# Two-layer streaming encoder step on one core: the embedding blocks' operands split into high and low parts

## The reference, cut to what matters

```python
def mixer_layer(h, p, ...):                       # two layers; 512 prompt frames and 8 x 16 sample frames
    z = rmsnorm(h, ln_in) @ w_in                  # 1024 -> 2464 columns: queries, latents, gates, conv inputs
    # o_a: latent attention, 8 heads; v: causal depthwise conv, width 31
    ...
    y_a = rmsnorm(o_a * silu(g_a), ln_out_a)
    v = silu(layernorm(v, ln_conv_g, ln_conv_b))
    y_c = rmsnorm(v * silu(g_c), ln_out_c)
    h = h + concatenate([y_a, y_c], axis=-1) @ w_out      # 1024 -> 1024
    gate = sigmoid(rmsnorm(h, ln_pg) @ w_pg)
    h = h + gate * (p @ w_pe)                             # p: 256 columns, the layer's input embedding
```

## Time and profile before

| | |
|---|---|
| three runs, us | 765.39, 765.08, 766.03 (median 765.39) |
| the profiled execution | 765.02 us, span 762.9 us |
| busy: TensorE / VectorE / ScalarE / GpSimd | 749.0 / 562.0 / 428.2 / 91.6 us |
| instructions | 10602 |
| TensorE's granted clock, mean | 0.996 of full |
| DMA | 70.69 MB, 92 GB/s to and from HBM over the span |

### The profile page before, as it was taken

One profiled execution on the slowest core, in us unless ns is written; L12 is line 12 of the kernel. 1 busy time (PEld: TensorE's weight loads), 2 busy tenths in 40 slices (PEclk: granted clock), 3 DMA queues, 4 the chain that ended last, 5 costly groups with the idle time before them and its releaser, 6 DMA issues.

```text
span 762.9 us, 10602 instructions
## 1 busy us (share of the span) xinstructions
PE 749.0 (98%) x3749; PEld 601.8 (79%) x3749; DVE 562.0 (74%) x1084; ACT 428.2 (56%) x996; POOL 91.6 (12%) x161
## 2 busy tenths in 40 slices
PE   9999999999999999999999999999999999999995
PEld 7899887767777588888888988877678767888874
DVE  3459978979877986546453798988888879655577
ACT  3865655665566733263366575647655758223564
POOL 1500323420001400000000020353000000000000
PEclk9999999999999999999999999999999999999998
DMA  8742222410011343412282223233111014332203
GB/s 271 229 128 83 88 73 86 115 36 15 35 35 28 123 167 130 134 56 83 66 279 77 91 76 85 82 81 83 41 36 43 1 54 154 110 125 74 88 5 138
DMA packets 50681, 70.69 MB, mean 93 GB/s; under 512 B 15582, under 2 KB 28154, under 8 KB 50614
## 3 DMA queue, kind: packets, MB, share of 16 engines
q1 hardware_dynamic: 44746, 59.27, 24.6%
q0 software_dynamic: 5824, 10.73, 5.2%
q10 hardware_dynamic: 60, 0.02, 0.0%
HBM read 60.79 MB, written 9.27 MB: 92 GB/s over the span
## 4 chain that ended last, share of the span: by engine, by line
PE 89%; DVE 6%; ACT 2%; DMA 1%; issue 1%; SPq 0%; POOL 0%; ACTq 0%
PE acc L692 20%; PE acc L701 20%; PE acc L698 19%; PE sharedT L616 5%; PE acc L836 5%; PE sharedS L930 4%; PE sharedO L944 4%; PE sharedO L616 2%; PE sharedS L616 2%; DVE VT L1623 2%; PE sharedT L902 1%; PE sharedS L888 1%; PE sharedO L874 1%; PE sharedS L889 1%; PE sharedO L913 1%
## 5 line engine op out<-in xcount | busy, mean ns | idle before, releaser
L692 PE MATMUL acc<-WHI,XHI 128*128 128x512 f32 (+1 forms) x710 | 304.7, 429 | 0.8 <-ACT WHI L1115 0.5
L701 PE MATMUL acc<-WHI,XLO 128*128 128x512 f32 (+1 forms) x710 | 274.7, 387 | 0.0
L698 PE MATMUL acc<-WLO,XHI 128*128 128x512 f32 (+1 forms) x710 | 274.3, 386 | 0.0
L1623 DVE SCALAR_TENSOR_TENSOR VT<-UX,CWT,VT 128x640 f32<-128x640 f32 x240 | 211.5, 883 | 5.0
L692 PEld LDWEIGHTS acc<-WHI,XHI 128*128 128x128 f32 x710 | 133.7, 188 | 29.8 <-issue 6.2
L1553 DVE SCALAR_TENSOR_TENSOR WLO<-WR,GT,WHI 128x512 fp32r<-128x512 f32 (+1 forms) x142 | 98.7, 737 | 78.8 <-ACT WHI L1115 78.6
L698 PEld LDWEIGHTS acc<-WLO,XHI 128*128 128x128 f32 x710 | 133.9, 189 | 27.3 <-issue 6.2
L701 PEld LDWEIGHTS acc<-WHI,XLO 128*128 128x128 f32 x710 | 133.3, 188 | 26.2
L1115 ACT ACTIVATE WHI<-WR,GT 128x512 fp32r<-128x512 f32 (+1 forms) x142 | 93.4, 708 | 85.5 <-PE acc L701 85.3
L1336 ACT ACTIVATE SB<-SB,NBIAS 128x128 f32<-128x128 f32 (+2 forms) x80 | 44.4, 555 | 37.0 <-DVE NBIAS L1682 35.6
L1115 ACT ACTIVATE PT<-sharedT 128x384 f32<-128x384 f32 (+1 forms) x80 | 35.6, 444 | 37.1 <-PE sharedT L616 36.9
(11 more groups left out here) (213 smaller groups left out, 884.4 us busy)
## 6 DMA issues: line engine op xcount, KB each, us to landing
WR<-in_w_in_dram SPq DMA_DIRECT2D x32, 256.0 KB, 3.1
WR<-in_w_in_dram SPq DMA_DIRECT2D x16, 512.0 KB, 3.7
WR<-in_w_out_dram SPq DMA_DIRECT2D x16, 512.0 KB, 3.7
WR<-in_w_pg_dram SPq DMA_DIRECT2D x16, 512.0 KB, 3.5
H<-in_x_prompt_dram SPq DMA_DIRECT2D x16, 256.0 KB, 5.2
WR<-in_w_in_dram SPq DMA_DIRECT2D x8, 416.0 KB, 5.8
residual_spill<-H SPq DMA_DIRECT2D x5, 512.0 KB, 3.4
H<-residual_spill SPq DMA_DIRECT2D x10, 256.0 KB, 3.4
```

What stands on the lines that cost most here:

```text
L692: mm(out, hi, w_hi, start=(first and k == 0), stop=False)
L698: mm(out, hi, w_lo, start=False, stop=False)
L701: last = mm(out, lo, w_hi, start=False, stop=(final and k == 1))
L1623: stt(out=out, in0=src, scalar=w, in1=out, op0=ALU.mult, op1=ALU.add).then_inc(conv_done, 1)
```

## The change

- `pe0` and `pe1` become quanta like all others: their chunks are parts (no gain), split by ScalarE and VectorE, and their inputs are split into rows 4 and 5 of `XHI` and `XLO`, which are free once part 2 of `gc` has been used. Three fp32r matmuls take the place of each plain one.
- The high parts of the inputs are two copies of 128x640 by ScalarE in unit 22; the low parts two subtractions of 128x640 by VectorE in units 27 and 29.
- `pe1` moves behind `oa0`. Parts are renumbered in each layer: 20 is `pe0`, 21 and 22 `oa0`, 23 `pe1`, 24 and 25 `oa1`, and so on, two higher than before from `oa1` on. Part 20 and 21 are split in the units 28 to 31.
- The turns of `y_a` stand between the tiles of `pe0` and of `oa0`'s first half.
- VectorE's and ScalarE's work after the attention is put in another order, and the table of taps is changed in "turn" and units 0, 2, 3, 24, 27.
- The load of a chunk waits for the split of the one three before, for `pe` too.

```diff
-BLOCKS = ["u0", "zA", "u1", "ga", "gc", "cv", "pe0", "pe1", "oa0", "oa1", "oc0", "oc1", "pg0", "pg1"]
+BLOCKS = ["u0", "zA", "u1", "ga", "gc", "cv", "pe0", "oa0", "pe1", "oa1", "oc0", "oc1", "pg0", "pg1"]
...
-PARTS = [c for c in CHUNKS if c[1][:2] != "pe"]
+PARTS = CHUNKS
...
-TAP["turn"] = _take(1)
-
-for _u, _m in enumerate((2, 1, 0, 4, 1, 1, 4, 2, 1, 2, 0, 2, 1, 1, 4, 2, 1, 2, 0, 2, 1, 1, 4, 1, 0, 1, 1, 3)):
+TAP["turn"] = _take(2)
+
+for _u, _m in enumerate((1, 1, 1, 3, 1, 1, 4, 2, 1, 2, 0, 2, 1, 1, 4, 2, 1, 2, 0, 2, 1, 1, 4, 1, 1, 1, 1, 2)):
     TAP[NB + _u] = _take(_m)
...
+        def first_x(name):
+
+            return 2 if name[:2] == "pe" else first_rows(name)
+
         def gain_column(i, k):
             l, name, c = PARTS[i]
+            if name[:2] == "pe":
+                return None
             col = G_IN if name in ZCOL else G_OUT if name[0] == "o" else G_PG
             col += 2 * (c + first_rows(name)) + k
             return GT[:, l, col:col + 1]
...
-                    pl, name, c = before = CHUNKS[j - RAW]
-                    if before in PART:
-                        sp.wait_ge(split_ready, PART[before] + 1)
-                    else:
-                        sp.wait_ge(acc_filled[TILES - 1], BLK[pl, name] + 1)
+                    before = CHUNKS[j - RAW]
+                    sp.wait_ge(split_ready, PART[before] + 1)
                 load_piece(sp, j)
...
-                    row = 2 * (c + first_rows(name)) + k
+                    row = 2 * (c + first_x(name)) + k
...
-
-            def embed(half, t, ks=(0, 1)):
-
-                j = CHUNK[l, f"pe{half}", 0]
-                if t == 0 and 0 in ks:
-                    raw_wait(pe, j)
-                if 0 in ks:
-                    pe.wait_ge(acc_drained[t], BLK[l, f"pe{half}"])
-                for k in ks:
-                    last = mm(acc[t][:, :], PTR[:, k, P * t:P * (t + 1)], WR[:, j % RAW, k, :],
-                              start=(k == 0), stop=(k == 1))
-                if 1 in ks:
-                    last.then_inc(acc_filled[t], 1)
...
-            copied_wait(pe, (l, "p2"))
-            embed(0, 0)
+            pe.wait_ge(p_low, 2 * (l + 1))
+            quantum("pe0", 0, 0)
             values(UNITS - 1)
-            for t in range(1, TILES):
-                embed(0, t)
-            embed(1, 0)
 
             def turn_ya(t):
                 pe.wait_ge(ya_ready, TILES * l + t + 1)
                 flip_half((l, ("y", t, 0)), Y[:, t, :])
 
             for t in range(1, TILES):
-                embed(1, t)
-                turn_ya(t - 1)
+                quantum("pe0", 0, t)
+                if t > 1:
+                    turn_ya(t - 2)
             for c in range(2):
                 for t in range(TILES):
                     copied_wait(pe, (l, ("y", t, 0)))
                     quantum("oa0", c, t)
-                    if (c, t) == (0, 0):
-                        turn_ya(TILES - 1)
+                    if c == 0 and t < 2:
+                        turn_ya(t + 3)
+            for t in range(TILES):
+                quantum("pe1", 0, t)
             for c in range(2):
                 for t in range(TILES):
...
+            def embeddings_high():
+
+                part_used(act, PART[l, "gc", 2])
+                for k in range(2):
+                    copy(XHI[:, :, 4 + k, :], PTR[:, k, :].rearrange("p (t e) -> p t e", e=P)).then_inc(p_high, 1)
...
                 split_high(NB + u)
+                if u == 22:
+                    embeddings_high()
+                if u in (28, 30):
+
+                    high(first_i + 20 + (u - 28) // 2)
...
             act.wait_ge(conv_done, CONVS * (l + 1))
-            for t in range(TILES):
-                embedding_out(0, t)
-                if t == 2:
-                    high(first_i + 20)
-            v_tanh_out(0)
-            for t in range(TILES):
+
+            def ya_square(t):
                 act.wait_ge(ya_ready, TILES * l + t + 1)
                 mean_square(Y[:, t, 0:512], 15 + t, 512)
+
+            embedding_out(0, 0)
+            embedding_out(0, 1)
+            ya_square(0)
+            embedding_out(0, 2)
+            high_half((l, ("y", 0, 0)))
+            ya_square(1)
+            embedding_out(0, 3)
+            high_half((l, ("y", 1, 0)))
+            embedding_out(0, 4)
+            high_half((l, ("y", 2, 0)))
+            high(first_i + 22)
+            high_half((l, ("y", 3, 0)))
+            ya_square(2)
+            high_half((l, ("y", 4, 0)))
+            ya_square(3)
+            ya_square(4)
+            v_tanh_out(0)
+            v_tanh_out(1)
+            high(first_i + 23)
+            v_tanh_out(2)
+            v_tanh_out(3)
+            for t in range(TILES):
+                embedding_out(1, t)
+                if t == 0:
+                    high(first_i + 24)
                 if t == 1:
-                    v_tanh_out(1)
-                embedding_out(1, t)
-                if t:
-                    high_half((l, ("y", t - 1, 0)))
-            high(first_i + 21)
-            high_half((l, ("y", TILES - 1, 0)))
-
-            for t in (2, 3, 4):
-                v_tanh_out(t)
+                    v_tanh_out(4)
             for t in range(TILES):
                 act.wait_ge(yc_ready, TILES * l + t + 1)
                 mean_square(Y[:, t, 512:1024], 20 + t, 512)
-            high(first_i + 22)
-            high(first_i + 23)
+            high(first_i + 25)
             for t in range(TILES):
...
-            for i in range(25, 28):
+                    high(first_i + 26)
+            for i in range(27, 30):
...
+                    if gain_column(i, k) is None:
+                        out = tt(split_place(i, 1, k, n), raw[:, k, :], split_place(i, 0, k, n).bitcast(F32), ALU.subtract)
+                        continue
...
+                if u in (27, 29):
+
+                    k = (u - 27) // 2
+                    dve.wait_ge(p_high, 2 * l + k + 1)
+                    tt(XLO[:, :, 4 + k, :], PTR[:, k, :].rearrange("p (t e) -> p t e", e=P),
+                       XHI[:, :, 4 + k, :].bitcast(F32), ALU.subtract).then_inc(p_low, 1)
+                if u >= 30:
+
+                    low(first_i + u - 10)
                 for t in CONV_OUT.get(u, ()):
                     conv_stats(t)
             sample_heads_out()
-            norm_of_conv()
             head_out(HEADS - 1)
             copied_wait(dve, (l, ("oh", HEADS - 1)))
             copied_wait(dve, (l, "oa"))
...
             for t in range(TILES):
                 y = Y[:, t, 0:512]
                 tt(y, y, OTOK[:, t, :], ALU.mult).then_inc(ya_ready, 1)
-            norm_of_conv_end()
-            for t in range(TILES):
-                normed(t)
-                if t == 2:
-                    low(first_i + 20)
-
             def conv_gate(t):
 
                 v = VT[:, 512 * t:512 * (t + 1)]
...
 
 
             low_half((l, ("y", 0, 0)))
+            norm_of_conv()
+            low_half((l, ("y", 1, 0)))
+            low_half((l, ("y", 2, 0)))
+            norm_of_conv_end()
+            low(first_i + 22)
+            low_half((l, ("y", 3, 0)))
+            normed(0)
+            low_half((l, ("y", 4, 0)))
+            normed(1)
             conv_gate(0)
-            for t in (1, 2, 3):
-                low_half((l, ("y", t, 0)))
-            conv_gate(1)
-            low_half((l, ("y", 4, 0)))
-            low(first_i + 21)
-            for t in (2, 3, 4):
-                conv_gate(t)
+            normed(2)
 
             def norm_of_y(group):
...
             norm_of_y(0)
-            low(first_i + 22)
+            low(first_i + 23)
             for t in range(TILES):
                 onto_residual("oa0", t)
-            low(first_i + 23)
+                if t in (1, 2):
+                    conv_gate(t)
+                    normed(t + 2)
+            low(first_i + 24)
+            conv_gate(3)
+            conv_gate(4)
+            low(first_i + 25)
             norm_of_y(1)
             for t in range(TILES):
                 low_half((l, ("y", t, 1)))
                 if t == 0:
-                    low(first_i + 24)
+                    low(first_i + 26)
                 if t > 1:
                     onto_residual("oa1", t - 2)
             onto_residual("oa1", 3)
             onto_residual("oa1", 4)
-            low(first_i + 25)
-            low(first_i + 26)
+            low(first_i + 27)
+            low(first_i + 28)
...
```

More of the change, by code:

```diff
@@ L311, in build @@
         p_in = sem("p_in")
+        p_high = sem("p_high")
+        p_low = sem("p_low")
         wq_rot = sem("wq_rot")
@@ L1471, in scalar_layer @@
                 if t == 0:
-                    high(first_i + 24)
-            for i in range(25, 28):
+                    high(first_i + 26)
+            for i in range(27, 30):
                 high(first_i + i)
@@ L1478, in scalar_layer @@
                 high_half((l, ("h", t, 0)))
-            high(first_i + 28)
+            high(first_i + 30)
```

(40 more changed lines are left out.)

## The result

The changed kernel takes **768.32 us** (median of 6 runs, 766.72 to 770.21), the kernel before 765.24 us (764.79 to 766.03); the ratio is 1.0038, 95% interval 1.0026 to 1.0050. It is slower by 0.4%. The time is inside the range that was given, but not in its likeliest case, which was no change (0.42): it is in the slower one (0.31). The profiled execution is the fastest of the six: 766.72 us around a span of 764.9 us.

What follows compares the result with a forecast made beforehand. TensorE's matmul stream was taken as the bound. A layer: -3.5 - 1.2 + 4.7 = 0.0, by the schedule's end +0.1; two layers +0.1 to +0.3, so 765.02 + 0.3 + 0.37 = 765.7 us; range 761.6 to 769.2.

Steps and rivals of the forecast that it cites:

- no change: Whole kernel: the time stays between 763.9 and 766.9 us; chance 0.42.
- the slower one: Whole kernel: slower than no change, rivals 2 and 3 taken together; chance 0.31.
- VectorE's schedule: VectorE after attention: a priced list of steps, 29 us of fixed work from 246.6 to 275.9 with one gap of 0.6.
- Matmuls and the small waits in them: Embeddings: ten tiles a layer at 1.37 instead of 1.72 us, -3.5 us; waits of 0.35 for low y4 and pe1's tile 0.
- Taps: Attention phase: moved taps close gaps in units 0 and 3 (-1.1 us), unit 27 gains 0.1; -1.2 us a layer.
- Added late units: Last attention units: added copies, subtractions and weight parts fit into idle time, cost 0; up to 2.5 us a layer kept for the range.
- The large waits: TensorE waits 1.4 and 2.1 us for drains in pe1's tiles 2 and 3, and 0.5 us for oa1's second part, a layer.
- the third rival: In pe1 the clock falls: tiles 2 to 4 at 1.2 GHz cost 4.1 us more a layer, 773.9 us; chance 0.03.
- The gain did not arrive: Rival 1 said oa0's drains come in time and the gain arrives: 756.3 us without waits, 761.0 with half; under 763.9, chance 0.27.
- Rival 2: Last units: a late weight part moves VectorE's list back; one part uncovered 768.3 us, both 770.7; chance 0.28.

Runs made afterwards that it cites:

- the run with drains and part 25: The changed kernel with VectorE's five drains of oa0 in a row and ScalarE's high part 25 ahead of the squares of lane 1: 757.77 us.
- the run that moves the subtraction: The run with drains and part 25, with VectorE's two low-part subtractions in units 29 and 30 instead of 27 and 29: 756.65 us, beside 757.83 us without the move.
- the runs with the clock held up: The changed kernel plus matmuls that compute nothing, ahead of pe1's tiles 2 and 3 (765.87 us) or ahead of tile 3 only (765.92 us).
- the run with the waits filled: The changed kernel plus matmuls that compute nothing, four ahead of pe1's tile 2 and seven ahead of its tile 3: 765.87 us.

## Why the prediction came out as it did

**The bound and the place: right.** VectorE's order makes TensorE wait in pe1's tiles 2 and 3 and in oa1, and that cancels the gain. VectorE's schedule held: products 3.25 us after pe0's start (245.91; 3.3 forecast), drain 3 at 273.69 (forecast 275.2 less 1.33, so 273.9).

**The terms, a layer, without the lower clock.** The sum was right within 0.2 us a layer, in part by luck, since errors of its parts cancel:

- *Matmuls and the small waits in them.* Forecast -3.5 and two waits of 0.35 for low y4 and pe1's tile 0, so -2.8. Measured between the start of pe0 and the end of oa1's tile 0 where the large waits are gone: 39.59 us (242.46, where that turn ends, to 282.05, the run with drains and part 25) against 42.10 (243.99 to 286.09), -2.5. The two waits make half of the difference: in that run they cost 0.50 and 0.35 us from start to start, not 0.35 each. The rest is spread over the turns and roundings.
- *Taps.* Forecast -1.2, measured -1.33, from two errors. The taps alone are worth 2.0: before the last units they gain 1.2, and in the last units 0.8 more, where I had 0.1. The subtraction that goes into unit 27 takes most of that back.
- *Added late units.* Forecast 0; measured +0.6 by the run that moves the subtraction (1.2 us in two layers), as the one in unit 27 stands ahead of a mask. I priced the subtraction where it replaces a tap and missed that it stands before the next mask. Its record is 0.82 us, as the Trainium skill's formula gives (VectorE: DVE Perf Modes, the TRN2 errata); from start to start it is 0.73 to 0.75, the price I took.
- *The large waits.* Forecast 1.4, 2.1 and 0.5, so 4.0. The brackets show 1.03, 1.78 and 0.44, counted from start to start they are 1.30, 2.06 and 0.71, so 4.07; the two runs that differ in them (765.87 and 757.77) give 8.1 / 2 = 4.05.

Together -2.5 - 1.3 + 4.05 = +0.2 a layer: 765.0 + 0.4 + 0.37 gives 765.8, and the runs with the clock held up took 765.87 and 765.92. The forecast for this case was 765.7.

**What failed: the third rival.** "No row shows a fall for such a wait. Chance 0.03." The mechanism was named, at the right place, with the wrong chance and the wrong size. That no row showed it was no evidence, since no wait of before was longer than about 0.8 us, but for 1.1 us ahead of its first matmul. Measured, a fall costs 1.7 us and not 4.1 us a layer: the profiled executions of five kernels have ten waits of 1.78 or 2.83 us and seven falls behind them, and the windows give 1.70 to 1.72 us for each, eight to nine matmuls and not three tiles of six. Where it pushes oa1 back, the wait of 0.44 us on part 25 disappears and 1.2 us net are left, as in layer 0 of the changed kernel (+1.53 us at oa1's tile 0, where the run with the waits filled has +0.3, its later start taken off). Two such falls are the 2.4 us of the median; that most executions have one or two is an estimate from their mean clocks. The Trainium skill (TensorE: Matmul & The Clock Gate, "HAM oscillation") describes a loop in which TensorE waits for a DMA in every round and starts each round's matmuls at half clock. The waits of that loop are longer than those of pe1, so the prediction's "by that rule the pe1 stretch would run slow" went further than the passage. The traces agree with it in that the clock falls with a wait. They differ in that 1.78 us were enough in some executions and not in others, and in that the work resumed at full clock and the fall came 0.4 to 1.5 us later. No row of before could give a chance; 0.03 treated the question as settled, and a larger one would have moved weight from no change to slower, 767 to 769.

**The other rivals.** The gain did not arrive, for the reason given. No late weight part held VectorE's list up before the drains: the products came in time (3.25 us). Rival 2's time, 768.3, is that of the result by luck, since the mechanism is another.

## What to carry to other kernels

When a change shortens a block of the bounding engine, lay out the queue of the engine that frees its buffers: drains that the next block waits for go first, work that is wanted later goes behind them, and then look for the next thing late on the third engine, here 2.8 us for a copy queued behind squares. A short step that is fitted into idle time of an engine is free only if nothing urgent is queued right behind it. A wait of TensorE costs more than its bracket, here by nearly 0.3 us each, and with the longer waits the clock; where such a wait can't be removed, it may be filled with matmuls into a bank that is rewritten later.

## What the runs showed of the hardware

- Behind a TensorE wait of 1.78 us (and of 2.83 us) the clock went to 1.2 GHz in some executions, for about eight matmuls of 0.43 us, and came back by itself while TensorE was busy. In the changed kernel it fell 1.5 us after the work had resumed (274.49, 276.0), in the seven falls 0.4 to 1.5 us after. The price was 1.7 us each time. Three of ten such waits, in the same executions, were followed by none. What decides that stayed open.
- Waits of about 1 us alone (11 runs), and gaps of TensorE filled with matmuls of no use, left the clock up. The scatter of a kernel's time mostly told it: 1.0 and 1.3 us with the long wait filled, 3.5 to 4.8 us with a long wait left, though only 1.9 us in the five runs of the split without the taps.
- A 128x512 matmul of the split kind takes 0.23 us from its start to the next in a row, and 0.34 us as the first behind a wait (274.49 to 274.83). Its record is 0.39 us long in a row, 0.16 us more than the step, and by that a wait's bracket is too short. The two together are the nearly 0.3 us.
